# First attention of a two-model kernel: two key tiles folded into one before the softmax, and parted by a mask after the transposition

## What is computed

```
rel  = qi + BLOCK - ki                      # qi in 0..127, ki in 0..255: the key tile before, then the own one
valid = (kpos >= 0) & (rel >= 0) & (rel < WINDOW)          # WINDOW = BLOCK = 128
logits = where(valid, q @ k * 64 ** -0.5 + bias, -1e30)
m = maximum(max(logits), sink)
e = exp(logits - m)
p = e / (sum(e) + exp(sink - m))
o = p @ v
```

## Time and profile before

| | us |
|---|---|
| median of 3 runs | 2614.54 (2613.16 to 2614.87) |
| the profiled execution, its own time | 2614.06 |
| its span in the trace | 2612.3 |
| TensorE busy | 2600.3 |
| VectorE busy | 1825.3 |
| ScalarE busy | 1373.6 |
| POOL busy | 80.1 |

### The profile page before, as it was taken

How to read it: one execution, slowest core, us unless ns; L and a number is a source line. 1 busy time by engine, 2 the same in 40 slices (tenths; PEclk the granted TensorE clock), 3 DMA queues, 4 the chain that set the end, 5 groups by cost and what they waited for, 6 DMA issues and landing times.

```text
span 2612.3 us, 35198 instructions
## 1 busy us (share of the span) xinstructions
PE 2600.3 (100%) x13652; PEld 2218.8 (85%) x13652; DVE 1825.3 (70%) x2455; ACT 1373.6 (53%) x2016; POOL 80.1 (3%) x142
## 2 busy tenths in 40 slices
PE   9999999999999999999999999999999999999999
PEld 7888888888888888888888888988888888888887
DVE  7876788887888786665665667676666567865665
ACT  5127766654444654454455446544555565445643
POOL 0000000000000000000000000010010001100100
PEclk9999999999999999999999999999999999999999
DMA  9995578788988686655655664565556656755563
GB/s 388 409 365 174 166 260 279 272 302 306 326 310 330 212 318 210 199 188 192 194 193 190 191 202 158 187 217 190 174 164 195 227 171 187 224 192 167 162 225 130
DMA packets 165367, 597.30 MB, mean 229 GB/s; under 512 B 19496, under 2 KB 20576, under 8 KB 164688
## 3 DMA queue, kind: packets, MB, share of 16 engines
q1 hardware_dynamic: 158832, 574.00, 64.5%
q0 software_dynamic: 6368, 21.04, 2.7%
HBM read 586.24 MB, written 3.49 MB: 226 GB/s over the span
## 4 chain that ended last, share of the span: by engine, by line
PE 93%; DVE 2%; ACT 2%; issue 1%; DMA 1%; SPq 0%; DVEq 0%; ACTq 0%
PE bank L846 28%; PE bank L888 28%; PE bank L900 14%; PE bank L851 14%; PE bank L863 2%; PE pS L863 1%; PE pX L863 1%; PE pX L995 1%; PE pS L934 1%; ACT both_w L1258 1%; DMA raw<-in_w_vw 1%; DVE both_w L1715 1%; PE pX L983 1%; PE pS L956 0%; PE pX L946 0%
## 5 line engine op out<-in xcount | busy, mean ns | idle before, releaser
L1715 DVE TENSOR_TENSOR both_w<-raw,both_w 128x1024 fp32r<-128x1024 f32 x848 | 1023.2, 1216 | 517.9 <-ACT both_w L1258 514.1
L1258 ACT ACTIVATE both_w<-raw 128x1024 fp32r<-128x1024 f32 x848 | 881.4, 1050 | 650.5 <-PE bank L851 398.2
L888 PE MATMUL bank<-H,both_w 128*128 128x512 f32 x3264 | 784.6, 391 | 0.1
L888 PEld LDWEIGHTS bank<-H,both_w 128*128 128x128 f32 x3264 | 598.8, 188 | 116.7 <-DVE XC L2250 0.9
L900 PE MATMUL bank<-H,both_w 128*128 128x256 f32 x3264 | 442.7, 285 | 0.5 <-DVE both_w L1715 0.5
L900 PEld LDWEIGHTS bank<-H,both_w 128*128 128x128 f32 x3264 | 424.5, 191 | 21.1 <-issue 1.7
L846 PE MATMUL bank<-both_w,H 128*128 128x512 f32 x1280 | 319.9, 392 | 1.1 <-DVE H L1718 0.6
L846 PEld LDWEIGHTS bank<-both_w,H 128*128 128x128 f32 x1280 | 237.9, 188 | 53.2 <-issue 2.7
L846 PE MATMUL bank<-both_w,F 128*128 128x512 f32 x1024 | 253.0, 389 | 0.0
L1767 DVE SCALAR_TENSOR_TENSOR raw<-raw,CR 128x1024 f32<-128x1024 f32 x192 | 231.8, 1217 | 11.9 <-DMA raw<-in_ada 11.4
L846 PEld LDWEIGHTS bank<-both_w,F 128*128 128x128 f32 x1024 | 192.1, 188 | 40.0
(11 more groups left out here) (352 smaller groups left out, 2210.1 us busy)
## 6 DMA issues: line engine op xcount, KB each, us to landing
raw<-in_w_in SPq DMA_DIRECT2D x280, 512.0 KB, 4.1
raw<-in_w_ff SPq DMA_DIRECT2D x256, 512.0 KB, 4.3
raw<-in_ada SPq DMA_DIRECT2D x192, 512.0 KB, 5.5
raw<-in_w_out SPq DMA_DIRECT2D x96, 512.0 KB, 4.7
raw<-in_w_vw SPq DMA_DIRECT2D x64, 512.0 KB, 4.3
raw<-in_w_sig SPq DMA_DIRECT2D x64, 512.0 KB, 4.9
raw<-in_w_x SPq DMA_DIRECT2D x32, 512.0 KB, 10.1
raw<-in_w_lru_out SPq DMA_DIRECT2D x32, 512.0 KB, 4.9
```

The lines of the kernel that those rows point to most:

```text
L888: ins = pe.matmul(out[i].rearrange("p (a s) -> p a s", a=2), whi[:, s, at_:at_ + 128], both[:, :, kt, :], start=(c == 0 and k == 0), stop= ...
L1258: act.activation(whi[:, s, 0:el.n], raw[el.slot][:, 0:el.n], ACT.Copy).then_inc(s_hi, 1)
L1715: dve.tensor_tensor(wlo[:, s, 0:n], raw[el.slot][:, 0:n], v32(whi[:, s, 0:n]), ALU.subtract).then_inc(s_lo, 1)
```

## The change

- DVE, `softmax`, second half only: after scale and bias, the two key tiles are combined by an element-wise maximum to a 128-wide tile (a new `tensor_tensor`, two heads in one instruction); the row maximum is then taken over 128 keys, not 256.
- ACT, `exps` and `weigh` work on 128 keys for the second half too.
- PE, `turn_both`: four transpositions rather than six, all to one PSUM bank (`pT`); the other (`pO`) is no longer used by it, nor waited for.
- ACT copies that bank in one instruction; the second copy (L1361) goes.
- DVE, new `banded(b)`: for the second half it multiplies the folded, transposed tile by a 0/1 mask into `PT[:, 1, 0:2]` (one key tile), then subtracts that from the folded tile in place (the other key tile). Each is a `tensor_tensor` over 128x256; the second waits for the first. `s_pt` now counts one step for ACT's copy and one for `banded`, and `values_both` waits for both. `banded(b-1)` stands in block b's iteration, at the tick between `softmax` of t = 1 and `inverse_both`.
- PE, `values_both`: the same six matmuls, from other places of `PT`.
- POOL builds the mask once, before the first bias load.

```diff
--- before.py
+++ after.py
@@ -489,6 +489,7 @@
     ones, ident, U = cst[:, C_ONE:C_ONE + 128], cst[:, C_ID:C_ID + 128], cst[:, C_U:C_U + 256]
     LP = at("LP", [128, 3, 2, S], o_lp)
     PT = at("PT", [128, 2, 4, 128], o_pt)
+    MASK = PT[:, 1, 2, :]
     BT = at("BT", [128, 2, 2, S], o_bt)
     SM = at("SM", [128, 4, 6, 2], o_sm)
     MX8 = at("MX8", [128, 2, 8], o_sm + 192)
@@ -960,14 +961,11 @@
         def turn_both(b):
 
             clear("T")
-            clear("O")
             pe.wait_ge(s_pw, 2 * b + 2)
             for t in range(2):
-                L = LP[:, (2 * b + t) % 3, :, :]
                 for i in range(2):
-                    for k in range(t + 1):
-                        o = pT[:, (2 * i + k) * 128:(2 * i + k + 1) * 128] if t else pO[:, 256 + 128 * i:384 + 128 * i]
-                        ins = pe.transpose(o, L[:, i, k * 128:(k + 1) * 128], ident)
+                    n = 2 * t + i
+                    ins = pe.transpose(pT[:, n * 128:(n + 1) * 128], LP[:, (2 * b + t) % 3, i, 0:128], ident)
             ins.then_inc(s_tr, 2)
             held["T"] = (s_pt, 2 * b + 2)
 
@@ -980,7 +978,7 @@
                 for i in range(2):
                     o = pO[64 * i:64 * i + 64, 128 * t:128 * t + 128]
                     for k in range(t + 1):
-                        ins = pe.matmul(o, heads[i][2][k], PT[:, 1 - t, (t + 1) * i + k, :], start=(k == 0), stop=(k == t),
+                        ins = pe.matmul(o, heads[i][2][k], PT[:, k, 2 * t * (1 - k) + i, :], start=(k == 0), stop=(k == t),
                                         skip_group_check=True)
             ins.then_inc(s_pv, 2)
             held["O"] = (s_o, 2 * b + 2)
@@ -1341,7 +1339,7 @@
             for advance in range(NB + 2):
                 if 0 <= advance - 1 < NB:
                     for t in range(2):
-                        weigh(2 * advance - 2 + t, 2 * advance - 2 + t, 128 * (t + 1))
+                        weigh(2 * advance - 2 + t, 2 * advance - 2 + t, 128)
                 yield
                 if advance >= 2:
                     b = advance - 2
@@ -1357,11 +1355,9 @@
                     act.wait_ge(s_tr, 2 * b + 2)
                     if b:
                         act.wait_ge(s_pv, 2 * b)
-                    act.activation(PT[:, 0, :, :], pT[:, :].rearrange("p (a q) -> p a q", q=128), ACT.Copy)
-                    act.activation(PT[:, 1, 0:2, :], pO[:, 256:512].rearrange("p (a q) -> p a q", q=128),
-                                   ACT.Copy).then_inc(s_pt, 2)
+                    act.activation(PT[:, 0, :, :], pT[:, :].rearrange("p (a q) -> p a q", q=128), ACT.Copy).then_inc(s_pt, 1)
                 if advance < NB:
-                    exps(2 * advance + 1, 2 * advance + 1, S, True)
+                    exps(2 * advance + 1, 2 * advance + 1, 128, True)
                 yield
                 yield
 
@@ -1899,6 +1895,10 @@
                 dve.scalar_tensor_tensor(out=L, in0=pS2[:, :, at_:at_ + nk], scalar=scale, in1=bias, op0=ALU.mult,
                                          op1=ALU.add).then_inc(s_lgt, 1)
             dve.wait_ge(s_lgt, a + 1)
+            if sink is not None and nk > 128:
+                k = vc.add(dve.tensor_tensor(L[:, :, 0:128], L[:, :, 0:128], L[:, :, 128:256], ALU.max))
+                dve.wait_ge(s_vc, k)
+                L = L[:, :, 0:128]
             if a >= 4:
                 dve.wait_ge(s_pw, a - 3)
             if sink is None:
@@ -1923,16 +1923,28 @@
             dve.wait_ge(s_vc, t)
             dve.reciprocal(rd, rs).then_inc(s_rd, 2)
 
+        def banded(b):
+
+            dve.wait_ge(s_gms, 4)
+            dve.wait_ge(s_pt, 2 * b + 1)
+            k = vc.add(dve.tensor_tensor(PT[:, 1, 0:2, :], PT[:, 0, 2:4, :], over(MASK, 2), ALU.mult))
+            dve.wait_ge(s_vc, k)
+            dve.tensor_tensor(PT[:, 0, 2:4, :], PT[:, 0, 2:4, :], PT[:, 1, 0:2, :], ALU.subtract).then_inc(s_pt, 1)
+
         def attention():
-            for b in range(NB):
+            for b in range(NB + 1):
                 yield from ticks(2)
                 for t in range(2):
-                    a, nk = 2 * b + t, 128 * (t + 1)
-                    dve.wait_ge(s_bt[b % 2], 32 * (b // 2 + 1))
-                    softmax(a, a, nk, SC1, BT[:, b % 2, :, 256 - nk:256], v(V_SINK + 2 * b, 2), 128 * t)
+                    if b < NB:
+                        a, nk = 2 * b + t, 128 * (t + 1)
+                        dve.wait_ge(s_bt[b % 2], 32 * (b // 2 + 1))
+                        softmax(a, a, nk, SC1, BT[:, b % 2, :, 256 - nk:256], v(V_SINK + 2 * b, 2), 128 * t)
                     yield
+                if b:
+                    banded(b - 1)
                 yield
-                inverse_both(b)
+                if b < NB:
+                    inverse_both(b)
                 yield
 
         def layer_jobs(l):
@@ -2409,6 +2421,10 @@
             pool.wait_ge(s_g, 16)
             pool.wait_ge(s_lg, 16)
             pool.wait_ge(s_ev["k"], 1)
+            pool.memset(MASK, 1.0).then_inc(s_gms, 1)
+            pool.wait_ge(s_gms, 3)
+            pool.affine_select(out=MASK, in_=MASK, pattern=[[-1, 128]], compare_op=ALU.is_ge, fill=0.0, base=127,
+                               channel_multiplier=-1).then_inc(s_gms, 1)
             load_bias(0)
             load_bias(1)
             for b in range(NB - 2):
```

## The result

The changed kernel takes 2618.62 us in the median of 22 runs, the kernel before 2614.12 us on the same occasions: 4.5 us more, a ratio of 1.0019 (changed over before, 95% interval 1.0013 to 1.0025). That is inside the 0.2% that I called no change, and on the slower side of 1. One of the 22 executions took 11538 us; without it the median is 2618.57, and the others lie between 2617.3 and 2620.1. The profiled execution took 2619.59 us, 1.0 above the median, with a span of 2617.9.

What follows compares the result with a forecast made beforehand. PE, busy throughout and 93% of the chain, was taken as the bound: waits +7.6 and transpositions -3.5 gave +4.1 us, 2618.2 for the profiled execution, 2618.6 us in the median; range 2614.5 to 2622.5.

Steps and rivals of the forecast that it cites:

- Transpositions, 3.5 us less: PE, `turn_both`: two fewer transpositions in each of 16 blocks, 0.109 us each, 3.5 us less PE work.
- The waits, 7.6 us: PE before `values_both`, waiting for `banded` in blocks 0, 2, 5, 7 and 8, plus 0.19 for the first fold: +7.6 us.
- block 3 went free: Block 3's values: `banded` done at 403.48 against PE's start at 403.91, the nearest block without a wait.
- The 0.27 that the prediction worked out from one element a cycle: DVE, float32 `tensor_tensor` of 256 elements at 0.96 GHz: estimated 0.27 us, its lower bound; the forecast took 0.42.
- the 0.19 us at the product of the earlier trace: Block 0: PE's product waiting for a lower-half split would wait 0.19 us longer for the first fold on DVE.
- "Costs nothing" for ScalarE and POOL: ACT's about 0.7 us less a block counted at nothing except in block 0; POOL's mask, built at the attention's start, nothing.
- The clock, a rival at 0.27: PE's clock halves in block 0's 3.0 us wait, costing 1.2 to 2.4 us more: 2620.4 us; chance 0.27.
- The base: The kernel before: profiled execution 2614.06 us, with the median taken as 0.48 above it.
- VectorE as the bound: Blocks 0 to 3 and 5 to 8: DVE's added 1.06 us a block carries over, one or two more waits, 2620.6; chance 0.13.
- The terms named for the upper end: Range's upper end, 2622.5 us: the clock at twice the stretch seen, and a wait more.
- the chances for "slower": Slower by over 0.2% (above 2619.8 us): 0.38, from 0.27 for clock and DVE cases and 0.10 for the own forecast.

Runs made afterwards that it cites:

- The run without the parting: Changed kernel with `banded` left out, values of the second query half using the folded tile for both key tiles: 2609.59 us, ratio 0.9984 to the kernel before.
- the place without the work: Kernel before, with block 0's values alone waiting for a tiny VectorE memset where `banded(0)` would stand: 2617.38 us, ratio 1.0014.
- Removing block 0's wait alone: Changed kernel with `banded` left out for block 0 only, its values taken from the folded tile: 2613.66 us, ratio 1.0000 to the kernel before.
- The parting a tick earlier: Changed kernel with ScalarE's copy of the turned tiles and `banded` one weight chunk earlier, all work done: 2609.60 us, ratio 0.9984 to the kernel before.
- the mask's product twice: Changed kernel with the product by the mask done twice in each block: 2621.66 us (5 runs), ratio 1.0033 to the kernel before.
- one interruption per block: Changed kernel with values, scores and turn at one tick; softmax, exponentials, inverse and weighing a tick later: 2617.22 us, ratio 1.0012 to the kernel before.

## Why the prediction held, point by point

- **Transpositions, 3.5 us less: right.** The run without the parting starts the last block's values 3.1 us earlier than before (627.30 against 630.44), having begun the first scores 0.3 later (309.50 against 309.19): 3.45 together.
- **The waits, 7.6 us: right in place and in size.** Predicted 3.0, 0.95, 1.36, 0.91, 1.19 for blocks 0, 2, 5, 7, 8, measured 3.06, 0.94, 1.36, 0.91, 1.16; block 3 went free, but by nothing, where the sum gave it 0.4. What carried it was the order on VectorE against starts in the trace, with a duration of 0.42 from the row of the same size. The 0.27 that the prediction worked out from one element a cycle would have been too low: the runs show 0.42. The Trainium skill's page "VectorE: DVE Perf Modes" has in its section on the TRN2 errata a formula with a fixed part for a float32 `tensor_tensor`, (N + 151) / 0.96 ns, which is an estimate of 0.42 for 256 elements; the trace agrees (419 to 425 ns). The exactness in hundredths is in part luck: `banded` starts 0.08 before the record of the split ends (347.63 against 346.49 + 1.22), where the sum lets it start behind, and the signal takes 0.15, not 0.07 (the earlier trace rows themselves give 0.09); the two cancel. One term was wrong: the 0.19 us at the product of the earlier trace rows did not come. VectorE had waited 0.41 us for ScalarE ahead of that split and waits 0.22 now, so the fold fitted into it.
- **"Costs nothing" for ScalarE and POOL: right.** No new wait names them.
- **The clock, a rival at 0.27, not in the forecast's sum: it happened.** In the profiled execution it cost 2.8 us, in that of the place without the work 1.5 (the next turn is 3.86 late, the values were 2.34 late). Removing block 0's wait alone gained 4.6 us in the medians, 1.6 more than the wait. So the clock belongs into the sum, at about 1.6 us in the median, and my forecast left it out. The rival's price, 1.2 to 2.4 us, was right for the median (and 0.4 short of the profiled execution). Its time, 2620.4, was not, for what follows.
- **What was on the other side.** Two things. The base: the sum began at 2614.54, the median of three runs, and the median of 22 is 2614.12, 0.4 lower. And the difference itself: waits 7.4, clock 1.6 and transpositions -3.5 make 5.5, and 4.5 was measured. The run without the parting shows 0.7 of the missing 1.0, being 4.2 us faster than the kernel before where its transpositions give 3.5. The chance wait near 793 may be what the changed kernels are spared (once in full and twice in part in four traces of the kernel before, never in eight of changed ones); this isn't settled.
- **VectorE as the bound: refuted.** The parting a tick earlier has all of VectorE's added work and no wait for it.
- **The range and the chances.** The terms named for the upper end, the clock at 2.4 and one wait more of about 1 us, reach 2622.0, not 2622.5, and the chances for "slower" add up to 0.37. Neither changes the reading.
- That the total came out to a tenth, with the clock left out on one side and the base and the missing 1.0 on the other, is luck; the places and lengths of the waits are not.

## What to carry to other kernels

Work that moves to an engine with room to spare costs what its place in that engine's queue costs. Compare, for each use, the end of what stands in front of the new work with the time at which the other engine will want it; where it is late, move it, and what it waits for, one step forward before weighing its size: here one step was worth 8.5 us and the operations themselves nothing. And count a wait of over 2 us on TensorE at more than its length, since the clock may fall: here by 1.6 us in the median.

## What I had not expected of the hardware

- Single waits amid dense products were followed by 0.50 of the clock (1.2 GHz): one of 2.3 us (0.50 for 3.4 us, 1.5 us lost), one of 3.1 (6.8 us, 2.8 lost), and one of about 3.6 with the mask's product twice (3.4 us). A wait of 2.7 us, in the run with one interruption per block, was not, nor was any of 1.9 or less. So the length alone doesn't decide, and the length of the fall doesn't follow it. The Trainium skill's page "TensorE: Matmul & The Clock Gate" (HAM oscillation) says that idle gaps between bursts of products bring the clock down, and names longer gaps than these; here a single one of 2.3 us did, and the measurement decides.
- Interrupting a stream of 128x512 products by one more group of small ones per block cost 0.2 us beyond the small ones' own time (3.24 us over 15 blocks). Joining the turn to the other two groups gained only 0.10 a block. So the same work in more groups is dearer, by 0.1 to 0.2 us a group here.
